# Layer norms of a feed-forward block: one pass over shifted rows, with sums, root and reciprocal by token on 128x4

## The reference, cut to what matters

```python
def _layer_norm(x, g, b):
    mu = jnp.mean(xf, axis=-1, keepdims=True)
    var = jnp.mean(jnp.square(xf - mu), axis=-1, keepdims=True)
    y = (xf - mu) * lax.rsqrt(var + NORM_EPS) * g + b

for l in range(DEPTH):                       # DEPTH = 2
    ...
    x = _layer_norm(DEEPNORM_ALPHA * x + g1 * y, ln1_g[l], ln1_b[l])
    h = x * (1 + sc2) + sh2
    x = _layer_norm(DEEPNORM_ALPHA * x + g2 * _sq_relu_mlp(h, w_fc1[l], w_fc2[l]), ln2_g[l], ln2_b[l])
    if not last:
        ...                                  # the same for xc
```

## Time and profile before

| | us |
|---|---|
| median of 3 runs | 1922.82 |
| lowest and highest run | 1918.45, 1926.38 |
| the profiled execution: its span, which is all the time that the page gives of it | 1922.7 |
| TensorE (PE) matmul busy | 1732.7 |
| VectorE (DVE) busy | 944.0 |
| ScalarE (ACT) busy | 644.2 |
| GpSimd (POOL) busy | 94.8 |

### The profile page before, as it was taken

The page is one execution under the profiler, slowest core; times in us unless marked ns, Lnnn a source line. Parts: engine busy times, 40 slices in busy tenths (PEclk is TensorE's granted clock), DMA queues, the critical chain, the costliest instruction groups (busy, mean ns, idle before and its releaser), DMA issues.

```text
span 1922.7 us, 22553 instructions
## 1 busy us (share of the span) xinstructions
PE 1732.7 (90%) x9106; PEld 1184.5 (62%) x9106; DVE 944.0 (49%) x1702; ACT 644.2 (34%) x1112; POOL 94.8 (5%) x136
## 2 busy tenths in 40 slices
PE   6988968999998779989988979999999798889998
PEld 5654733444676334447545658888888574578886
DVE  5573310002444000135576555888675757755555
ACT  2155121122231111123356535322222424655443
POOL 0790000000000000000000000000000100000000
PEclk8998988999999889999998989999999999999999
DMA  9977499999948999992100112454454130024540
GB/s 386 392 306 318 174 414 410 421 421 421 397 187 324 403 410 420 417 397 86 68 23 1 37 51 88 153 207 188 185 209 175 44 119 35 23 88 176 177 174 22
DMA packets 62899, 430.04 MB, mean 224 GB/s; under 512 B 6592, under 2 KB 10816, under 8 KB 10944
## 3 DMA queue, kind: packets, MB, share of 16 engines
q1 hardware_dynamic: 62784, 428.48, 56.0%
HBM read 427.40 MB, written 1.05 MB: 223 GB/s over the span
## 4 chain that ended last, share of the span: by engine, by line
PE 64%; DVE 15%; DMA 11%; ACT 7%; issue 2%; SPq 1%; ACTq 0%; DVEq 0%
PE bank L292 14%; PE bank L1100 12%; PE bank L296 9%; PE bank L297 8%; PE bank L298 8%; DMA ring<-in_ws_dram 7%; DMA work<-in_ws_dram 3%; DVE ring_halves L2495 3%; ACT work_halves L2489 2%; PE bank L331 2%; PE bank L2134 1%; DVE work L438 1%; PE bank L2111 1%; PE bank L2593 1%; PE bank L2519 1%
## 5 line engine op out<-in xcount | busy, mean ns | idle before, releaser
L296 PE MATMUL bank<-work_halves 128*128 128x512 f32 (+1 forms) x1088 | 396.6, 365 | 27.8 <-DVE HH_halves L2924 8.5
L298 PE MATMUL bank<-work_halves,ring_halves 128*128 128x512 f32 (+1 forms) x1088 | 386.7, 355 | 0.0
L297 PE MATMUL bank<-HH_halves,work_halves 128*128 128x512 f32 (+1 forms) x832 | 287.3, 345 | 0.0
L1100 PE MATMUL bank<-ring,work 128*32 128x512 f32 (+2 forms) x896 | 258.1, 652 | 17.1 <-DMA work<-in_ws_dram 9.6
L1100 PE MATMUL bank<-work 128*32 128x512 f32 (+2 forms) x640 | 222.2, 653 | 38.6 <-DMA ring<-in_ws_dram 36.7
L296 PEld LDWEIGHTS bank<-work_halves 128*128 128x128 f32 x1088 | 207.9, 191 | 64.6 <-DVE HH_halves L2924 14.9
L298 PEld LDWEIGHTS bank<-work_halves,ring_halves 128*128 128x128 f32 x1088 | 207.6, 191 | 28.6
L2495 DVE TENSOR_TENSOR ring_halves<-ring,work_halves 128x2048 fp32r<-128x2048 f32 x72 | 163.6, 2289 | 55.5 <-ACT work_halves L2489 55.5
L297 PEld LDWEIGHTS bank<-HH_halves,work_halves 128*128 128x128 f32 x832 | 159.9, 192 | 20.4 <-issue 2.2
L1378 DVE TENSOR_TENSOR work<-work,bank 128x512 f32<-128x512 f32 x14 | 9.6, 688 | 298.6 <-PE bank L1100 298.6
L1100 PEld LDWEIGHTS bank<-work 128*32 128x32 f32 (+2 forms) x640 | 62.3, 138 | 136.7 <-issue 134.1
(11 more groups left out here) (368 smaller groups left out, 2570.5 us busy)
## 6 DMA issues: line engine op xcount, KB each, us to landing
ring<-in_ws_dram SPq DMA_DIRECT2D x287, 1024.0 KB, 10.3
work<-in_ws_dram SPq DMA_DIRECT2D x117, 1024.0 KB, 18.4
con<-in_con_dram SPq DMA_DIRECT2D x1, 1177.0 KB, 27.3
XX<-in_xT_dram SPq DMA_DIRECT2D x1, 1024.0 KB, 9.8
XX<-in_cT_dram SPq DMA_DIRECT2D x1, 1024.0 KB, 22.0
out_dram<-XX SPq DMA_DIRECT2D x1, 512.0 KB, 3.6
out_dram<-XX SPq DMA_DIRECT2D x2, 256.0 KB, 2.6
par<-in_par_dram SPq DMA_DIRECT2D x1, 338.0 KB, 3.0
```

Source lines behind the costliest of these rows:

```text
L296: pe.matmul(out, l[0], r[0], start=start, stop=False)
L297: pe.matmul(out, l[0], r[1], start=False, stop=False)
L298: return pe.matmul(out, l[1], r[0], start=False, stop=stop)
L1100: m = pe.matmul(b[c, :], left[:, k, c], ring_of(self.w[i])[:, 512 * k:512 * k + 512], start=first and k == 0, stop=last and k == 3, skip_g ...
```

## The change

The norm becomes one pass over rows from which an estimate has been taken. The estimate, `shift`, is a quarter of the mean of the first two chunks' sums: their 256 features are summed by two ones-matmuls (`pe_shift`) and scaled by 1/256. Chunks 0 to 3 get it subtracted after their result is made (`dve_less`); for chunks 4 to 7 it is subtracted from the old state ahead of the product (`dve_ready`), and the product is then added straight out of PSUM (`dve_direct`), without ACT's eviction. The sum and the sum of squares of the shifted rows come by `pe_sums`: per chunk and per 128 tokens one matmul with the data as the weights and one column of ones, so that token t's sum lands on partition t of one column; four columns for 512 tokens, two for 256, in bank 7 (sums) and bank 6 (squares). Mean, variance, root and reciprocal are then on 128x4 (128x2), and TensorE spreads the reciprocal `rs` and the product `dr` (mean times rs) back to 128 x n, with a broadcast column as the weights and the identity. Per chunk DVE multiplies by rs (`dve_scaled`) and subtracts dr (`dve_normed`), both out of PSUM, and makes h; ACT makes the high half from the state itself with h's gain and bias rather than from h. Sqrt's table is loaded ahead by a one-element root. The splits of weight chunks 4 and 5 stand earlier, among the products; in B the splits 0 and 1 of mix1's weights move within the last additions. The core of the diff:

```diff
+                st.wait_ge(eng, "h", k, q)
...
-                    ro.take("var", 1)
+                    ro.put(3, "rs", 1)
+                    ro.put(5, "dr", 1)
...
+            def pe_shift(self, pe, v, o):
+                st, n = self.st, self.n
+                st.wait_ge(pe, "res", v, o)
+                if v == 1 and o == 0:
+                    st.wait_ge(pe, "variance", 0)
+                t = pe.matmul(bank[6][:, 0:n], ones, XX[:, o, 0:n], start=o == 0, stop=o == 1)
+                if o == 1:
+                    t.then_inc(st.pe("shift sum", v), 1)
+
+            def pe_sums(self, pe, v, o):
+                st = self.st
+                st.wait_ge(pe, "no sums", v)
+                st.wait_ge(pe, "less", v, o)
+                for t in range(self.n // P):
+                    m = pe.matmul(bank[7][:, t:t + 1], XX[:, o, P * t:P * t + P], ones[:, 0:1], start=False, stop=o == 7, skip_group_check=True)
+                if o == 7:
+                    m.then_inc(st.pe("sum", v), 1)
+                st.wait_ge(pe, "square of", v, o)
+                st.wait_ge(pe, "no squares", v)
+                for t in range(self.n // P):
+                    m = pe.matmul(bank[6][:, t:t + 1], self.dev[:, o, P * t:P * t + P], ones[:, 0:1], start=False, stop=o == 7, skip_group_check=True)
+                if o == 7:
+                    m.then_inc(st.pe("sum of squares", v), 1)
+
             def pe_norm(self, pe, v):
-                st, n = self.st, self.n
-                b = bank_of(pe, st, self.ro, "var", v)
-                for k in (0, 1):
-                    st.wait_ge(pe, "square of", v, k)
-                    pe.matmul(b[:, 0:n], ones, self.dev[:, k, 0:n], start=k == 0, stop=False)
-                for k in (2, 4, 6):
-                    st.wait_ge(pe, "dev", v, k)
-                    t = pe.matmul(b[:, 0:n], ones, self.dev[:, k, 0:n], start=False, stop=k == 6)
-                t.then_inc(st.pe("var", v), 1)
-
-            def pe_sum(self, pe, v, o):
-                if o >= 0:
-                    st, n = self.st, self.n
-                    st.wait_ge(pe, "res", v, o)
-                    if v == 1 and o == 0:
-                        st.wait_ge(pe, "mu", 0)
-                    t = pe.matmul(bank[6][:, 0:n], ones, XX[:, o, 0:n], start=o == 0, stop=o == 7)
-                    if o == 7:
-                        t.then_inc(st.pe("sum", v), 1)
+                st = self.st
+                for name, cols in (("rs", self.rt4), ("dr", self.dr)):
+                    b = bank_of(pe, st, self.ro, name, v)
+                    st.wait_ge(pe, name, v)
+                    for t in range(self.n // P):
+                        m = pe.matmul(b[:, P * t:P * t + P], cols[:, t:t + 1].broadcast_to([P, P]), ident, start=True, stop=True)
+                    m.then_inc(st.pe("spread", name, v), 1)
...
+                            if (o, k) == (7, 5):
+                                self.pe_sums(pe, 0, 6)
...
-                        self.pe_sum(pe, 0, o - 2)
-                self.pe_sum(pe, 0, 6)
-                self.pe_sum(pe, 0, 7)
+                        if o in (1, 2):
+                            self.pe_shift(pe, 0, o - 1)
+                        for i in {5: range(4), 6: (4, 5)}.get(o, ()):
+                            self.pe_sums(pe, 0, i)
+                self.pe_sums(pe, 0, 7)
                 self.pe_norm(pe, 0)
...
-                    self.pe_sum(pe, 1, 6)
-                    self.pe_sum(pe, 1, 7)
+                    for o in (5, 6, 7):
+                        self.pe_sums(pe, 1, o)
                     self.pe_norm(pe, 1)
...
-                        self.pe_sum(pe, 1, o - 2)
+                        if o in (1, 2):
+                            self.pe_shift(pe, 1, o - 1)
+                        for q in {5: range(4), 6: (4,)}.get(o, ()):
+                            self.pe_sums(pe, 1, q)
...
+            def act_squares(self, act, v, os):
                 st, n = self.st, self.n
-                for k in range(8):
-                    st.wait_ge(act, "centred", v, k)
-                    act.activation(self.dev[:, k, 0:n], XX[:, k, 0:n], ACT.Square).then_inc(st.act("square of", v, k), 1)
-                if v == 0:
-                    self.split_act(act, 5)
-                st.wait_ge(act, "var", v)
-                act.activation(self.mu[:, 0:n], bank[self.ro.of["var", v][0]][:, 0:n], ACT.Sqrt, scale=1.0 / 1024, bias=EPS).then_inc(st.act("evicted", ("var", v)), 1)
+                for o in os:
+                    st.wait_ge(act, "less", v, o)
+                    act.activation(self.dev[:, o, 0:n], XX[:, o, 0:n], ACT.Square).then_inc(st.act("square of", v, o), 1)
+
+            def act_root(self, act, v):
+                st = self.st
+                st.wait_ge(act, "variance", v)
+                act.activation(self.root4, self.va, ACT.Sqrt, bias=EPS).then_inc(st.act("root of", v), 1)
...
+                self.split_act(act, 4)
+                self.act_squares(act, 0, range(4))
+                self.split_act(act, 5)
+                self.act_squares(act, 0, range(4, 8))
+                self.act_root(act, 0)
...
+                    st.wait_ge(act, "normed", 0, k)
+                    for q in range(self.nq):
+                        t = act.activation(r_(self.X[0][:, 512 * k + 256 * q:512 * k + 256 * q + 256]), XX[:, k, 256 * q:256 * q + 256], ACT.Identity,
+                                           scale=self.gh[:, k, q:q + 1], bias=self.bh[:, k, q:q + 1])
+                    t.then_inc(st.act("xh", k), 1)
+                    st.wait_ge(act, "xh", k)
                     st.wait_ge(act, "h", k)
-                    act.activation(r_(self.X[0][:, c]), self.X[1][:, c], ACT.Copy).then_inc(st.act("xh", k), 1)
...
+                            if i == 34:
+                                act.activation(small[:, 248:249], ones[:, 0:1], ACT.Sqrt)
...
+            def dve_shift(self, dve, v):
+                st, n = self.st, self.n
+                st.wait_ge(dve, "shift sum", v)
+                dve.tensor_scalar(self.shift[:, 0:n], bank[6][:, 0:n], 1.0 / 256, None, MUL).then_inc(st.dve("shift row", v), 1)
+                st.wait_ge(dve, "shift row", v)
+                dve.memset(bank[6][:, 0:4], 0.0).then_inc(st.dve("no squares", v), 1)
...
+            def dve_ready(self, dve, v, os):
+                st, n = self.st, self.n
+                for o in os:
+                    st.wait_ge(dve, "shift row", v)
+                    if v == 0:
+                        t = dve.scalar_tensor_tensor(out=XX[:, o, 0:n], in0=XX[:, o, 0:n], scalar=ALPHA, in1=self.shift[:, 0:n], op0=MUL, op1=SUB)
+                    else:
+                        st.wait_ge(dve, "evicted", ("fc2", 6, o))
+                        t = dve.tensor_tensor(XX[:, o, 0:n], XX[:, o, 0:n], self.shift[:, 0:n], SUB)
+                    t.then_inc(st.dve("ready", v, o), 1)
+
+            def dve_direct(self, dve, o):
+                st, mod = self.st, self.M.mod
+                st.wait_ge(dve, "out", o)
+                st.wait_ge(dve, "ready", 0, o)
+                for q in range(self.nq):
+                    c = slice(256 * q, 256 * q + 256)
+                    t = dve.scalar_tensor_tensor(out=XX[:, o, c], in0=bank[self.ro.of["out", o][0]][:, c], scalar=mod[:, 16 + o, q:q + 1], in1=XX[:, o, c], op0=MUL, op1=ADD)
+                t.then_inc(st.dve("evicted", ("out", o)), 1)
+                st.at["less", 0, o] = st.at["evicted", ("out", o)]
...
+                dve.tensor_scalar(self.de, bank[7][:, 0:m], 1.0 / 1024, None, MUL).then_inc(st.dve("mean", v), 1)
...
+                dve.tensor_tensor(self.d2, self.de, self.de, MUL).then_inc(st.dve("mean square", v), 1)
...
+                dve.scalar_tensor_tensor(out=self.va, in0=bank[6][:, 0:m], scalar=1.0 / 1024, in1=self.d2, op0=MUL, op1=SUB).then_inc(st.dve("variance", v), 1)
...
+                dve.reciprocal(self.rt4, self.root4).then_inc(st.dve("rs", v), 1)
...
+                dve.tensor_tensor(self.dr, self.de, self.rt4, MUL).then_inc(st.dve("dr", v), 1)
...
+            def dve_scaled(self, dve, v, k):
...
+                    dve.tensor_tensor(XX[:, k, 0:n], XX[:, k, 0:n], bank[self.ro.of["rs", v][0]][:, 0:n], MUL).then_inc(st.dve("scaled", v, k), 1)
...
+                dve.tensor_tensor(XX[:, k, 0:n], XX[:, k, 0:n], bank[self.ro.of["dr", v][0]][:, 0:n], SUB).then_inc(st.dve("normed", v, k), 1)
...
+                self.dve_no_sums(dve, 0)
+                self.dve_result(dve, 0)
+                self.dve_result(dve, 1)
+                self.split_dve(dve, 2)
+                self.dve_result(dve, 2)
+                self.dve_shift(dve, 0)
+                self.dve_less(dve, 0, (0, 1, 2))
+                self.dve_result(dve, 3)
+                self.split_dve(dve, 3)
+                self.dve_less(dve, 0, (3,))
+                self.dve_ready(dve, 0, (4, 5))
+                self.split_dve(dve, 4)
+                self.dve_direct(dve, 4)
```

(21 more changed lines are left out.)

127 lines of the change are left out of this document (76 added, 51 removed).

## The result

The changed kernel takes 1942.86 us (median of 4 runs, 1941.02 to 1952.83) against 1920.63 for the one before on the same chips: ratio 1.0128, 95% interval 1.0110 to 1.0146, so 21 to 28 us slower, 24.6 by the ratio (the two medians alone are 22.2 apart). Forecast was 1934, slower, range 1916 to 1944.

The account below looks back on a forecast made before the run. TensorE was taken to bound the kernel, with 53 us of holes at three norms within reach. An unchanged clock gave -4.4 us; with clock losses the sum was +12.4, 1935, put at 1934 for partly hidden slow starts; range 1916 to 1944.

Parts of the forecast that it names:

- hole B: TensorE's gap in the norm after ffn0's fc2: 18.7 us to become 10.4, plus 2.2 for slow sums.
- M: Stretch from mix1 up to ffn1's out-projection: +2.0 us, from seven DVE steps longer by 0.29.
- hole A: TensorE's gap in ffn0's norm after the out-projection, before fc1: 20.7 us to become 8.2.
- hole C: TensorE's gap in ffn1's norm (256 tokens), before fc1: 13.9 us to become 7.
- D: From ffn1's fc1 to its next products: weight split 6 waits behind eight longer DVE steps, +1.3 us.
- B's DVE step: DVE's time per chunk behind ffn0's fc2 norm: 2.01 to 2.3 us with dr's subtraction and no POOL disturbance.
- the second rival: Behind ffn0's fc2 norm POOL still disturbs DVE: step 2.7 us, +2.9, total 1937; chance 0.12.
- The clock: Prediction's list of clock losses in sums around the norms: +6.0 twice, +1.3 twice, +2.2; what follows starts slow as before.
- The clock falls in a one-column piece: Sums 0 to 3 in one piece behind product o=5: clock falls 2.9 us in, +6.0 us in each ffn0 norm.
- The first rival: One-column matmuls hold the clock at 1.00 as wide ones do; total 1918 us; chance 0.18.
- Added work ahead of the holes: One-column sums replacing wide ones before the three norms' TensorE gaps: +9.3, +5.9 and +4.7 us at full clock.
- Splits and table at nothing: Weight splits 4 and 5 moved among the products, and Sqrt's early table load: no gain or cost.

Follow-up runs that it names:

- low_on_dve: The changed kernel with mix1's low half of the second 256 tokens behind ffn0's fc2 made by DVE instead of POOL; ratio 1.0097 to the kernel before.
- no_dr_b: The changed kernel with dr subtracted on only 4 of 512 columns in the norm after ffn0's fc2; ratio 1.0100 to the kernel before.
- spread_sums: The changed kernel with each chunk's one-column sums placed between wide matmuls of products o=5 to o=7, not in one piece; ratio 1.0039 to the kernel before.
- the twins: Two kernels adding idle matmuls to the kernel before behind product o=5 of each norm: one-column, ratio 1.0150, or wide (512 columns, 256 in ffn1), 1.0084.
- piece_narrow: The kernel before with idle one-column matmuls, read by nobody, added behind product o=5 of all three norms; ratio 1.0150 to the kernel before.
- no_sums: The changed kernel without the one-column matmuls of chunks 0 to 6 in all three norms; ratio 0.9893 to the kernel before.
- split_table: The kernel before with only Sqrt's table loaded ahead and weight split 5 moved forward behind product o=6; ratio 0.9996 to the kernel before.

## Why the prediction was right and wrong

The table sets the terms of the sum beside what three executions measured against the kernel before. Up to hole B and in C the three run the same code, so the differences between them tell how far one execution can be trusted (in M they don't: low_on_dve leaves out POOL's part, no_dr_b the subtraction).

| part | forecast | changed | low_on_dve | no_dr_b |
|---|---|---|---|---|
| A up to its hole | +16.6 | +18.0 | +18.0 | +18.0 |
| hole A | -12.5 | -12.2 | -9.9 | -9.7 |
| fc1, fc2 and B's sums up to hole B | +11.9 | +8.5 | +12.4 | +11.8 |
| hole B | -6.1 | -5.0 | -6.2 | -6.3 |
| M, behind hole B | +2.0 | +6.5 | +6.4 | +3.0 |
| C up to its hole | +6.0 | +8.0 | +6.5 | +5.0 |
| hole C | -6.9 | -4.1 | -4.2 | -5.2 |
| D | +1.3 | +1.2 | +1.2 | +1.2 |

- **The first step that failed is B's DVE step, mis-sized**: 2.30 forecast, 2.82 measured, so "Seven steps longer by 0.29 give back 2.0" where the stretch behind hole B grew by 5.9 us and stage M by 6.5. The subtraction was counted: it takes 0.71 from start to start where 0.62 was put, and taking it out gave 0.54 a step back (no_dr_b). The 0.5 missed are POOL's: I let its disturbance vanish because low_x now waits for h; it moved from h to DVE's own low_x, which takes 0.86 of the step and not 0.33. That was the second rival (0.12, with 2.7 a step); it came true beside the first forecast, not in its place.
- **The second is the list under "The clock"**, the line "What follows starts slow as before". It priced the clock ahead of the holes and in B's last sums, and let the spread, g2 and all other matmuls in the holes run at full clock. In C the spread took 2.08 us for 8 instructions (0.94 for 8 in the sum) and g2 3.62 (1.88 in before): hole C 9.8, 9.7 and 8.7 in the three executions for 7. Not all of that is the clock: in spread_sums, at 0.82, it was 8.5. In A the changed kernel's profiled execution had luck (8.5, at 1.00); in the other two the spread took 3.78 and the hole 10.8 and 11.0 for 8.2. In B the spread took 3.78 as well, but of the last sums, priced at 2.2, only the last eight instructions ran slow (+0.8), and the hole, forecast at 12.6 with them, was 13.7, 12.5 and 12.4.
- **The clock falls in a one-column piece**: right. It fell 2.9 us in (2.9 was taken) in A, instructions doubled, and product o=6 began at 0.52. In B it fell 5.0 us in, and 2.2 and 2.4 us in in the other two executions. The first rival, clock up, had 0.18 and is refuted by the twins. The rule read from the Trainium skill (TensorE: Matmul & The Clock Gate, What's actually happening), clock by how busy TensorE has been, taken by its word, does not agree with piece_narrow: busy 10.10 of 10.10 us, clock 0.76 and then 0.68. One of the prediction's rows for this was weaker than it was made to be: TensorE had been busy since 1042.4, in part with 512-column matmuls (L292), when the stretch from 1048.2 to 1051.6 showed 0.50, and the clock came back at its very end. That narrow matmuls lose the clock is shown by the twins and not by that row.
- **Added work ahead of the holes**: right. The one-column sums of chunks 0 to 6 were 29.8 us of the sum; spread_sums less no_sums measured 28.
- **C's weight split behind longer DVE steps**: right, 1.3 forecast and 1.2 measured (D). What C cost beyond its forecast is its hole, and in the changed kernel's profile the slow start of its out-projection, which the other two executions of the same code don't have.
- **Splits and table at nothing**: no run shows otherwise. split_table holds split 5 and the table's load, and its time is that of before within 3 us; split 4 wasn't tried alone.

The measured 1942.86 lies inside the range, near its high end, and that is in part luck. The high end was built from dearer clock terms ahead of the holes; what carried the time there were the longer DVE step behind B and the clock inside the holes, neither of which it allowed for.

## What to carry to other kernels

A reduction to one column is short in the instruction list, and here it was still a stretch in which TensorE lost its clock: 7.2 us of it at full clock took 9 to 11, and the next product and the next chain paid too. The same matmuls in portions of 1.8 us among wide ones kept 1.00 up to the holes, but their 28 us of work remained; the ones-matmul that costs 0.88 a chunk was cheaper than eight one-column matmuls at 1.8. When a clock fall is in a forecast, price every instruction until it comes back, and profile more than one execution: where the clock fell moved single stages by 2 to 4 us. When an extra operation is put on a loop that a second engine disturbs, don't count on the disturbance to go: here it moved to the next operation.

## What the hardware showed unexpectedly

- Constant wide matmuls in idle time held the clock at 1.00 through 20.7 and 18.6 us holes, and this won 2.7 us behind one of three holes (stage B 372.1 for 374.8; M and C unchanged).
- DVE's low_x on 128x256 takes 0.41 us alone and 0.94 when POOL's has just begun; two in a row on DVE take 0.75. Here POOL's help cost DVE more than doing the work itself. In the kernel before DVE's began 0.05 us ahead of POOL's and took 0.42, and the next operation, h, was the one that was stretched.
